# New PSUM banks for chunk 1's results and the first tokens, pointwise slabs earlier in the weight order, three late turns, and chunk 0's attention on 43 quarters instead of 27

## The reference, cut to what matters

```python
h = _rmsnorm(x, g_mix)
a, gate, q, k, v = split(h @ w_in)            # 512, 512, 8x64, 8x64, 8x64 columns
u = a * sigmoid(gate)
c = causal depthwise conv of u, 31 taps       # 512 channels
c = silu(layernorm(c)) @ w_pw                 # the pointwise projection
q, k = per-head rmsnorm(q), rmsnorm(k)
z = q.k / 8;  A[t,s] = sigmoid(z) * prod_{s<j<t} (1 - sigmoid(z_j)),  s < t
x = x + concat(c, A @ v) @ w_out
x = x + relu(rmsnorm(x) @ w_ff1)**2 @ w_ff2   # 4096 hidden columns
```

## Time and profile before

| | us |
|---|---|
| median of 3 runs | 2836.68 (2835.9 to 2837.76) |
| the profiled execution | 2836.54 |
| its span, first to last instruction | 2834.8 |
| PE busy | 2706.6 |
| DVE busy | 1672.9 |
| ACT busy | 1069.4 |

### The profile page before, as it was taken

The page is one execution under the profiler, slowest core; times in us unless marked ns, Lnnn a source line. Parts: engine busy times, 40 slices in busy tenths (PEclk is TensorE's granted clock), DMA queues, the critical chain, the costliest instruction groups (busy, mean ns, idle before and its releaser), DMA issues. The chain is left out here.

```text
span 2834.8 us, 37422 instructions
## 1 busy us (share of the span) xinstructions
PE 2706.6 (95%) x13872; PEld 2273.7 (80%) x13872; DVE 1672.9 (59%) x2653; ACT 1069.4 (38%) x2144; POOL 453.2 (16%) x460
## 2 busy tenths in 40 slices
PE   7878789999999899999999999999999999999999
PEld 6756677788888788778888797778888887898998
DVE  6986776657773468357775357736888842212222
ACT  4333523456552212345554212244666630221221
POOL 2211210012220011022322002102333310000000
PEclk9999899999999999999999999999999999999999
DMA  9695597777777658465554846854455456353542
GB/s 315 236 342 180 166 357 261 288 254 272 273 264 299 243 197 278 174 246 182 179 185 163 315 166 207 268 208 154 139 189 188 144 178 256 138 204 134 195 162 93
DMA packets 262047, 616.19 MB, mean 217 GB/s; under 512 B 23217, under 2 KB 159409, under 8 KB 213741
## 3 DMA queue, kind: packets, MB, share of 16 engines
q1 hardware_dynamic: 261869, 613.80, 60.8%
HBM read 444.79 MB, written 168.94 MB: 217 GB/s over the span
## 5 line engine op out<-in xcount | busy, mean ns | idle before, releaser
L1973 PE MATMUL ps<-h2T_hi,w_s 128*128 128x512 f32 (+1 forms) x1280 | 465.1, 363 | 7.8 <-DMA w_s<-w_scratch 3.7
L1142 POOL TENSOR_TENSOR beta<-beta,stay 128x512 f32<-128x512 f32 (+3 forms) x328 | 312.9, 954 | 906.6 <-DVE stay L1819 870.6
L1975 PE MATMUL ps<-h2T_hi,w_s 128*128 128x512 f32 (+1 forms) x1280 | 453.8, 355 | 0.0
L1974 PE MATMUL ps<-h2T_lo,w_s 128*128 128x512 f32 (+1 forms) x1280 | 453.7, 354 | 0.0
L1889 DVE TENSOR_TENSOR resid<-ps,resid 128x512 f32<-128x512 f32 x256 | 174.7, 688 | 261.2 <-PE ps L2231 260.6
L1414 ACT ACTIVATE stay<-ps 128x512 f32<-128x512 f32 (+3 forms) x328 | 174.8, 533 | 370.5 <-PE ps L2169 215.2
L2229 PE MATMUL ps<-w_s,hid_hi 128*128 128x512 f32 x768 | 308.5, 402 | 0.0
L2230 PE MATMUL ps<-w_s,hid_lo 128*128 128x512 f32 x768 | 299.9, 390 | 0.0
L2231 PE MATMUL ps<-w_s,hid_hi 128*128 128x512 f32 x768 | 299.8, 390 | 0.0
L1489 ACT ACTIVATE ps<-ps 128x512 f32<-128x512 f32 (+1 forms) x160 | 81.3, 508 | 558.0 <-PE ps L1975 558.0
L1973 PEld LDWEIGHTS ps<-h2T_hi,w_s 128*128 128x128 f32 x1280 | 242.8, 190 | 39.6 <-DMA w_s<-w_scratch 3.8
(11 more groups left out here) (211 smaller groups left out, 5208.6 us busy)
## 6 DMA issues: line engine op xcount, KB each, us to landing
w_s<-w_scratch SPq DMA_DIRECT2D x282, 1024.0 KB, 7.9
w_scratch<-w_s SPq DMA_DIRECT2D x94, 1024.0 KB, 8.9
w_raw<-in_w_ff SPq DMA_DIRECT2D x64, 512.0 KB, 5.5
a_k<-k_scratch SPq DMA_DIRECT2D x80, 256.0 KB, 3.9
a_v<-v_scratch SPq DMA_DIRECT2D x80, 256.0 KB, 4.1
a_q<-q_scratch SPq DMA_DIRECT2D x64, 256.0 KB, 4.6
w_raw<-in_w_in SPq DMA_DIRECT2D x20, 512.0 KB, 7.7
mix_scratch<-ohl SPq DMA_DIRECT2D x66, 128.0 KB, 2.9
```

The costliest lines, as they stand in the source:

```text
L1142: nc.gpsimd.tensor_tensor(v[0:q.r, 0:n], v[0:q.r, 0:n], stay_of(q.z)[0:q.r, 1:n + 1], ALU.mult).then_inc(s_a, 1)
L1973: nc.tensor.matmul(out, w[0], x[0], start=start, stop=False)
L1974: nc.tensor.matmul(out, w[0], x[1], start=False, stop=False)
L1975: return nc.tensor.matmul(out, w[1], x[0], start=False, stop=stop)
```

## The change

`front`'s banks become fixed by kind: ag results keep place modulo three, event s takes bank 2 or 0 by turns, and both halves of a turn take bank 1, one after the other (the second two slots later, on PE and on ACT). An event then waits for the event before last. The first tokens' transposes of tiles 0 to 2 go to three pairs of banks, and PE waits for a low part six halves back in place of two; DVE makes three norms ahead and splits slab 0 between the low parts of tiles 1 and 2. The two pointwise slabs stand behind ag slab 1 in the weight order, in place of behind ag slab 5. q result 1 (event 9) is turned in `out(0)` too. Attention of chunk 0 ends before slot 74 (43 slots) in place of 58, and the mixed activations are loaded at slots 76, 78, 80 and 82 in place of 62, 66, 71 and 75 (the gain row for the next norm follows three slots behind the last of them, as before). Turned results are stored 12 slots behind their event in place of 10.

```diff
-MIX_AT = (62, 66, 71, 75)
+MIX_AT = (76, 78, 80, 82)
...
 def att_past(c):
-    return 58 if c == 0 else 116
+    return 74 if c == 0 else 116
...
-            before = pw_slot(0) // 4 + 1
             front = [(sec, 1, j) for sec, _, j in proj]
-            w += proj + front[:before] + [("pw", 0, j) for j in range(2)] + front[before:]
+            w += proj + front[:2] + [("pw", 0, j) for j in range(2)] + front[2:]
...
         def norm_bank(which, c, i, hf):
-            return 4 + hf if which else (2 * i + hf) % 3 if c == 1 else 6 + hf
+            return 4 + hf if which else (2 * i + hf) % 3 if c == 1 else (6, 0, 2, 6)[i] + hf if c == 0 else 6 + hf
         def norm_back(which, c):
-            return 3 if c == 1 and not which else 2
+            return 2 if which or c > 1 else 3 if c else 6
...
-        OUT_TURN, OUT_TURNED = (10, 11), (6, 7)
+        OUT_TURN, OUT_TURNED = (9, 10, 11), (6, 7)
...
+        def front_bank(kind, x, q=0):
+            return x % 3 if kind == "ag" else (2, 0)[x % 2] if kind == "event" else 1
+
+        def front_free(kind, x, q=0):
+            if kind == "turn":
+                return kqT_ok, 2 * (8 + kvq_events(1)[x][2]) + q
+            if kind == "event":
+                return taken(1, x - 2) if x >= 2 else (ag_u, 8) if x else (ag_sig, 7)
+            if x < 3:
                 return ag_u, 4
+            return (ag_u if x % 2 else ag_sig), 4 + (x - 3) // 2 + 1
...
-                        if t == event_out(s) + 10 and s not in OUT_TURN:
+                        if t == event_out(s) + 12 and s not in OUT_TURN:
                             store_turned(1, s)
...
-                    if c == 0 and s in (2, 3):
+                    if c == 0 and 2 <= s < 2 + len(OUT_TURN):
                         store_turned(1, OUT_TURN[s - 2])
...
-                        if t == event_out(s) + 9 and sec != "v" and s not in OUT_TURN:
-                            kvq_turned(1, s, [front_bank("turn", s, q) for q in range(2)])
+                        for q in range(2):
+                            if t == event_out(s) + 9 + 2 * q and sec != "v" and s not in OUT_TURN:
+                                kvq_turned(1, s, [front_bank("turn", s)] * 2, (q,))
...
-            norm_scale(0, 0, 0)
+            for i in range(3):
+                norm_scale(0, 0, i)
             for i in range(4):
-                if i < 3:
-                    norm_scale(0, 0, i + 1)
                 norm_lo(0, 0, i)
+                if i == 0:
+                    norm_scale(0, 0, 3)
+                if i == 1:
+                    splits_until(-2.0)
             splits_until(0.0)
...
-                        if t == KVQ_AT + 4 * (s + 3) and sec != "v" and s not in OUT_TURN:
-                            for q in range(2):
+                        for q in range(2):
+                            if t == event_out(s) + 8 + 2 * q and sec != "v" and s not in OUT_TURN:
                                 pe.wait_ge(*front_free("turn", s, q))
                                 turn_packed(1, s, q, front_bank("turn", s, q))
...
-                    pe.wait_ge(kqT_ok, 28)
+                    pe.wait_ge(kqT_ok, 2 * (16 - len(OUT_TURN)))
...
-                        if c == 0 and ev < 2:
+                        if c == 0 and ev < len(OUT_TURN):
                             turn_both(1, OUT_TURN[ev], OUT_TURNED)
```

More of the change, by code:

```diff
@@ L668, in late_taps @@
             return range(min(TAPS, TAPS - LATE[c] + 2 * slot), min(TAPS, TAPS - LATE[c] + 2 * slot + 2))
[L672 to L689, removed]
-                return ag_u, 4
[L691 to L696, removed]
+        def front_bank(kind, x, q=0):
[6 more added lines that the diff above has]
+            if x < 3:
+                return ag_u, 4
+            return (ag_u if x % 2 else ag_sig), 4 + (x - 3) // 2 + 1
         def ln_step(c, slot):
@@ L1290, in kvq_high, with kvq_turned @@
                                    kn[0:r, m % 2, :].rearrange("p (h d) -> p h d", h=NH)).then_inc(pk_hi, 1)
-            def kvq_turned(c, s, banks):
+            def kvq_turned(c, s, banks, halves_of=(0, 1)):
                 sec, i, m = kvq_events(c)[s]
@@ L1297, in kvq_turned @@
                     return
-                if m >= 2:
+                if m >= 2 and 0 in halves_of:
                     act.wait_ge(kq_st[m % 2], kq_stores(c, m - 2))
-                for q in range(2):
+                for q in halves_of:
                     act.wait_ge(kqT_ps, 2 * (8 * c + m) + q + 1)
```

## The result

The changed kernel takes 2861.27 us (median of 4 runs, 2858.8 to 2866.26) against 2836.29 us for the kernel before on the same chip: ratio 1.009, 95% interval 1.0078 to 1.0102, some 25 us slower. The forecast was 2834, with 2821 to 2847 as the range.

What follows compares the result with a forecast made beforehand. It took DVE to be late in attention pressed into 27 slots, with three banks making PE wait. Output's second half at 396.9 instead of 403.55, plus 3 and 1, gave -2.65 us: forecast 2834 us, range 2821 to 2847.

Steps and rivals of the forecast that it cites:

- part 2: Front, pointwise slabs sooner: ACT and DVE wait at the tenth result; net 0.7 us won, bounds 5.8 won to 4 lost.
- the first piece of part 4: Slots 38 to 57: DVE busy 0.85 instead of 0.72, so 57.6 us; at 0.72 the projections end at 388.5.
- part 4: Attention on 43 slots with new banks: 114.1 us from first queries to projections' end at 377.7, 20.5 us sooner.
- Part 1: First tokens: first matmul at 20.6 us instead of 23.3, 2.5 us won; bounds 0 to 2.7.
- part 3: Eight slabs k0 to v3 issued at slot 32: first queries land 26.4 us later, at 263.6; bounds 3 us either way.
- part 5: Before output, mixed loads behind the last result: output's second half begins 19.2 us after the projections' end, at 396.9.
- low clock and late turn: After the wait before output: half clock costs 3 us, the third late turn adds 1 us to output.
- The rule quoted in the prediction: Repeating gaps on the engine that should be full can mean too little buffer space; all gaps close: 2824 us, chance 0.25.
- The rival on the slower side: Wait before output costs its full 13.9 us and 4 more, attention stays as it is: 2845 us, chance 0.22.

Runs made afterwards that it cites:

- I: Kernel before with only the new opening (own banks for three tiles' first tokens, three norms ahead, first slab split between the lows); ratio 0.9984.
- A: Changed kernel with only the old order of the weight slabs put back; ratio 1.0009 to the kernel before.
- C: Changed kernel with the old slab order, attention on 27 slots and mixed activations loaded at the old slots; ratio 0.9984.
- B: Changed kernel with only chunk 0's attention back on 27 slots and mixed activations loaded at slots 62, 66, 71 and 75; ratio 1.0063.
- N: G with ACT copying each half turn one slot sooner, in the slot in which PE makes it; 2821.32 us, ratio 0.9947.
- G: A with the mixed activations loaded at slots 76 to 79, ahead of the four output slabs; 2825.7 us, ratio 0.9958.
- K: Kernel before with the new opening, attention on 43 slots and early mixed loads, keeping three shared banks and two late turns; 2834.2 us, ratio 0.9988.
- M: Changed kernel with SP's pointwise stores and slab loads of the front's first nine slots behind chunk 0's last two query stores; ratio 1.0106.

## Why the prediction was wrong, point by point

Forecast and kernel after differ by 26.7 us in the profiled execution. Two of the prediction's steps failed by about as much, part 2 (13.2 us, far outside its bounds) and the first piece of part 4 (13.2 us, near the end of its bounds). The second only left out a gain that was forecast; the first belongs to the slab order, which the runs show to be nearly all of the loss. The split by the prediction's own steps:

| step | forecast | measured | late by |
|---|---|---|---|
| slot 12 of the front (200.0 less 2.5 and 0.7 of parts 1 and 2) | 196.8 | 210.7 | 13.9 |
| slot 12 to slot 38 (part 3) | 66.8 | 67.3 | 0.5 |
| slots 38 to 57 (part 4) | 57.6 | 70.8 | 13.2 |
| slots 58 to 73 | 47 | 45.0 | -2.0 |
| slots 74 to 79 | 9.5 | 9.3 | -0.2 |
| projections' end to output's second half (part 5) | 19.2 | 22.2 | 3.0 |
| low clock and late turn (all that is left to the end) | 4 | 2.4 | -1.6 |

The forecast counts from the first queries' landing; slot 38's scores began 2.4 us before its first projection matmul, so by the scores the second row would be 2.4 us less and the third as much more.

**Part 1 was right.** The first projection:

```profile
20.59 0.50 PE L1964 MATMUL ps<-hT_hi,w_s 128*128 128x512 f32 x1 [1.98 <-DVE hT_lo L1584]
```

Forecast 20.6; alone, in I, it was worth 2.5 us at the output.

**Part 2 is the step that failed.** Its waits were right (12.6 us on ACT for 12, 8.55 on DVE for 7.5), its balance was not: "the last q store comes sooner, and `csq` with it". The copy for that store did come sooner, the store 7.5 us later. The prediction named the pointwise stores and the loads of ag 2 to 5 that stand before it, and gave them no price. What was missing is one look at the DMA column: from 145 to 184 us the kernel before runs its DMA engines at 1.01 to 1.02. In such a stretch ACT's stop of 12.6 us, which keeps SP at ACT's copies and the engines half idle, puts off 2.0 MB, and the pointwise stores put 2.1 MB more in front of the last queries; DVE's idle time won back elsewhere pays none of it. Slot 12 came 13.9 us later than forecast: with part 1 as it was, part 2 lost 13.2 us, against bounds of 5.8 won to 4 lost.

**Part 3 was right in size**, and hid its meaning. From slot 32's issue at 250.64 to the scores of slot 38 at 275.6 it took 25.0 us; forecast 26.4 to the landing. But the prediction set this beside the kernel before, where twelve attention steps (it says thirteen) fill the same slots. A shows what seven steps and early k slabs would have taken: 14.5 us from slot 31 to 38 instead of 25.2. With slot 38 at 254.6 in A and 278.0 in the kernel after, the slab order costs 23.4 us by there.

**Part 4 was half right.** Attention on 43 slots is worth 14 us at the projections' end (A against C, after against B), and `raw_kq` went. Slots 58 to 73 ran with DVE busy 0.98, as forecast (0.97). Slots 38 to 57 did not run at the 0.85 taken, in the kernel after and in A alike. First slots 38 to 57, 58 to 73 and 74 to 79 of the kernel after, then slots 31 to 37 and the same three stretches of A:

```profile
278.00:348.80 70.80, 57.05 (x294) 46.99 (x294) 50.78 (x99) 35.72 (x92) 20.16 (x22) 0.90 0.59 186
348.80:393.80 45.00, 36.12 (x172) 28.98 (x171) 43.99 (x75) 22.47 (x50) 7.95 (x9) 0.92 0.63 203
393.80:403.10 9.30, 9.29 (x45) 7.33 (x43) 9.30 (x17) 2.29 (x4) 3.84 (x2) 1.00 0.78 279
```

```profile
240.10:254.60 14.50, 13.69 (x71) 11.13 (x70) 8.22 (x19) 5.64 (x17) 3.40 (x5) 1.00 0.93 357
254.60:325.00 70.40, 55.16 (x295) 45.35 (x294) 52.28 (x102) 37.03 (x95) 22.40 (x24) 0.93 0.60 187
325.00:369.90 44.90, 35.88 (x172) 28.91 (x171) 43.90 (x75) 22.49 (x50) 7.87 (x9) 0.92 0.63 202
369.90:379.10 9.20, 9.20 (x45) 7.33 (x43) 9.20 (x16) 2.29 (x4) 3.92 (x2) 1.00 0.76 279
```

DVE is busy 50.78 of 70.8 us in the kernel after, 0.72, and 52.28 of 70.4 in A, 0.74: the prediction's bound (0.72), not its 0.85; by its own terms that bound ends the projections at 388.2, not the 388.5 it states. The prediction saw the banks that were added and not that all turns now share one, whose second half waits for ACT's copy; N took 5.5 us less there than G, so the turn bank is at most a part of the 13.2, and the rest stays open. The rule quoted in the prediction from the Trainium skill, "Perfetto Trace Analysis", Identifying Performance Opportunities, has its limit here: the new banks moved the repeating gap from `raw_kq` to `kqT_second` (10.5 us before, 12.6 after; 11.2 in K, 12.5 in G). It closed when the instruction that frees the bank came one slot sooner.

**Part 5 was right in kind and 3.0 us short.** SP's queue and PE at the output:

```profile
403.12 1.95 SPq L727 DMA_DIRECT2D w_raw<-in_w_out  x4
405.11 0.48 SPq L824 DMA_DIRECT2D q_scratch<-kqT_late  x1
405.63 6.13 SPq L826 DMA_DIRECT2D q_scratch<-kqT_late  x2
411.86 2.52 SPq L929 DMA_DIRECT2D mix_first_hi<-mix_scratch  x1
...
415.54 0.38 SPq L929 DMA_DIRECT2D mix_first_lo<-mix_scratch  x1
```

```profile
408.62 0.77 PE L2322 MATMUL ps<-w_s,mix_first_hi 128*128 128x512 f32 x1 [5.54 <-DMA mix_first_lo<-mix_scratch]
...
425.31 0.79 PE L2322 MATMUL ps<-w_s,mix_first_hi 128*128 128x512 f32 x1 [12.25 <-DMA mix_first_lo<-mix_scratch]
```

As forecast, four slab loads and the late turn's store stand before the last two loads. Not forecast: the first two, planned for slots 76 and 78, had not landed either (5.54 us of wait), since SP had stood 7.9 us for attention's last stores and issued them only at 400.28 and 400.75; and the late turn's store held SP for 6.1 us.

The rival on the slower side, 2845 from a projections' end later than 380.3, named this wait and attention unimproved; it happened, but the larger cause lay earlier. Had slot 12 been put 13.9 us later and slots 38 to 79 at the 125.1 us they took in place of 114.1, the forecast would have been 2858.9.

## What to carry to other kernels

Before moving a load earlier, look at how busy the DMA engines are in the stretch where its consumer will now stand: where they are full, a stop that keeps the issuing engine from issuing is paid in bytes later, and so is every store that moves in front of what is waited for; M's other order of the queue did not help. A slab loaded sooner also holds its buffer longer; count whose load is put off by that. And a new buffer is worth only what the instruction that empties it allows: look for who frees it, and how soon.

## What was not expected of the hardware

An issue of two stores of 256 KB held SP for 11.43 us with the DMA engines full (at 181.00 in the kernel after), while the same pair took 1.88 us in M, at 178.13, when they were at 0.67 of their time (170 to 184 us). Seven slab transfers of 1 MB had been issued in the 9 us before the slow pair and none in the 30 us before the fast one, so whether the full engines or the transfers waiting ahead count is not separated. All issues behind the slow pair, of other transfers too, waited with it. The granted clock from 403.0 to 425.3 was 0.70, between its two levels, 1.2 and 2.4 GHz: the first twelve matmuls after the wait of 5.54 us took 4.44 us (408.62 to 413.06), where the kernel before took 2.99 for the same twelve (400.69 to 403.68).
